# Last four experts that write finished rows, 64-row products in half chunks and 16-token tiles paired, in a one-core float32 hybrid layer

## The reference

```python
n = rms_norm(h, norm1_g)
u = n @ w_in
h = h + (sigmoid(g0) * (y_rwkv @ w_p_rwkv)       # 384 channels
       + sigmoid(g1) * (y_sb   @ w_p_sb)         # 320 channels
       + sigmoid(g2) * (y_fox  @ w_p_fox)) @ w_out   # 320 channels
t = rms_norm(h, norm2_g)
g_idx = argmax(t @ wg + bg)                      # one of 4 groups
top_v, top_i = top_k(le_sel, 2)                  # two of the 4 experts in that group
for e in range(16):
    he = silu(t @ w_gate[e]) * (t @ w_up[e])
    y = y + combine[:, e:e + 1] * (he @ w_down[e])
out = h + y
```

## Time and profile before

| | |
|---|---|
| median of 3 runs | 1109.23 us (1108.11 to 1111.26) |
| profiled execution, its own time | 1108.83 us |
| its span in the profile | 1107.0 us |
| mean granted TensorE clock | 0.956 of full speed |
| PE / PEld busy | 1012.5 us (91%) / 597.7 us (54%) |
| DVE / ACT / POOL busy | 317.9 / 211.6 / 84.8 us |
| moved by DMA | 111.52 MB |

### The profile page before, as it was taken

The page is one execution under the profiler, slowest core; times in us unless marked ns, Lnnn a source line. Parts: engine busy times, 40 slices in busy tenths (PEclk is TensorE's granted clock), DMA queues, the critical chain, the costliest instruction groups (busy, mean ns, idle before and its releaser), DMA issues.

```text
span 1107.0 us, 15412 instructions
## 1 busy us (share of the span) xinstructions
PE 1012.5 (91%) x6388; PEld 597.7 (54%) x6388; DVE 317.9 (29%) x672; ACT 211.6 (19%) x462; POOL 84.8 (8%) x196
## 2 busy tenths in 40 slices
PE   5997998998998879999999999999999669999992
PEld 4885776876766644555554444443345434444441
DVE  3213553223123157222222333333310342212110
ACT  4002321120210252233320000060012201101100
POOL 7700000000000000000000000000000011121211
PEclk9997999999999999999998999999999779999997
DMA  7212012101000200311110111043360347999994
GB/s 200 62 58 76 1 41 37 50 3 50 2 2 2 60 1 20 96 39 38 38 38 19 39 38 38 1 173 92 114 247 38 152 152 221 345 350 340 358 283 115
DMA packets 104262, 111.52 MB, mean 101 GB/s; under 512 B 16305, under 2 KB 93233, under 8 KB 104129
## 3 DMA queue, kind: packets, MB, share of 16 engines
q1 hardware_dynamic: 99584, 93.76, 26.4%
q0 software_dynamic: 4608, 16.78, 6.0%
HBM read 97.40 MB, written 15.20 MB: 102 GB/s over the span
## 4 chain that ended last, share of the span: by engine, by line
PE 87%; DVE 5%; issue 3%; ACT 2%; DMA 2%; SPq 0%; POOL 0%; DVEq 0%; POOLq 0%; ACTq 0%
PE ps L1356 15%; PE ps L1571 10%; PE ps L1258 8%; PE ps L1204 7%; PE ps L1185 7%; PE ps L1498 6%; PE ps L1528 5%; PE ps L1585 5%; PE ps L1209 5%; PE ps L1424 2%; PE ps L1457 2%; PE ps L1458 1%; PE ps L1563 1%; PE ps L1483 1%; PE ps L1435 1%
## 5 line engine op out<-in xcount | busy, mean ns | idle before, releaser
L1356 PE MATMUL ps<-arena 128*128 128x512 f32 x384 | 185.1, 623 | 1.0 <-ACT yT_all L626 0.3
L1356 PEld LDWEIGHTS ps<-arena 128*128 128x128 f32 x384 | 71.2, 197 | 73.3 <-issue 72.0
L1258 PE MATMUL ps<-arena 64*64 64x64 f32 x2376 | 82.3, 223 | 12.6 <-DVE arena L861 10.8
L1258 PEld LDWEIGHTS ps<-arena 64*64 64x64 f32 x2376 | 75.3, 137 | 33.5 <-issue 25.5
L1204 PE MATMUL ps<-arena 128*128 128x264 f32 x320 | 84.4, 408 | 0.0
L1571 PE MATMUL ps<-arena 128*128 128x512 f32 x176 | 78.7, 598 | 2.0 <-issue 1.9
L465 POOL DMA_INDIRECT arena<-n_rows,idx x16 | 15.6, 978 | 842.0 <-DVE idx L1067 834.1
L1185 PE MATMUL ps<-arena 128*128 128x264 f32 x320 | 73.1, 388 | 1.2 <-PE ps L1185 1.2
L1498 PE MATMUL ps<-yT_all,arena 128*128 128x512 f32 x144 | 68.0, 614 | 0.0
L1185 PEld LDWEIGHTS ps<-arena 128*128 128x128 f32 x320 | 60.6, 191 | 13.5 <-issue 2.8
L1204 PEld LDWEIGHTS ps<-arena 128*128 128x128 f32 x320 | 59.5, 195 | 12.4 <-issue 0.7
(11 more groups left out here) (318 smaller groups left out, 1103.5 us busy)
## 6 DMA issues: line engine op xcount, KB each, us to landing
arena<-in_moe_w_down SPq DMA_DIRECT2D x16, 1024.0 KB, 13.1
arena<-in_w_in SPq DMA_DIRECT2D x24, 512.0 KB, 3.9
arena<-in_moe_w_gate SPq DMA_DIRECT2D x11, 1024.0 KB, 14.4
arena<-in_moe_w_up SPq DMA_DIRECT2D x11, 1024.0 KB, 17.6
arena<-in_w_in SPq DMA_DIRECT2D x9, 1024.0 KB, 5.3
yT_all<-in_moe_w_gate SPq DMA_DIRECT2D x5, 1024.0 KB, 14.6
yT_all<-in_moe_w_up SPq DMA_DIRECT2D x5, 1024.0 KB, 17.0
arena<-in_w_out SPq DMA_DIRECT2D x1, 4096.0 KB, 13.5
```

The costliest lines, as they stand in the source:

```text
L1258: ins = mm(psf[q, 512 * bank + c * CH:512 * bank + (c + 1) * CH], lhs(q, c), rhs(q, c), start=True, stop=True)
L1356: ins = mm(ps[:, 5 + 2 * (n % 2), :], gate_w[:, (n + 1) % 4, c, :], nT[:, c, META:L], start=(c == 0), stop=(c == DC - 1))
```

## The change

1. **V tiles.** The four 128-token tiles of both pieces come first. The two 16-token tiles become one last group, "tail", of 16 steps: in each pair of steps one product goes to PSUM partitions 0 to 15 (320 columns) and one to 32 to 47 (325 columns), of the same bank.
2. **Projection.** Six banks instead of two. In each block, the seven products with 128 rows come first; then the two 64-row chunks as four products of 256 tokens, b = 1 and b = 2 in turn.
3. **Experts in time.** `ORDER` = 0, 4, 8, 12, 1, 5, 9, 13, 2, 6, 10, 14, 3, 7, 11, 15. The last four belong to four different groups.
4. **The end.** Twelve experts are added as before. When the twelfth has landed, ACT issues the copy of `y_dram` to `out`. For each of the last four, POOL gathers the rows so far from `y_dram` (`sums_in`), DVE multiplies and adds (`y_final`, two of 512 columns), and POOL writes the rows to `out` (`final_rows`), the first of them after the copy has landed.
5. **Other edits.** `down` signals its lower half by itself (`down_low`). `tables()` stands behind `rows_T(1)` and `gated(0)`, its two copies from PSUM before `rows_T(0)`. Head sums share two semaphores, and the wait for `qg8_ready` and `tilde_ready` go. The runtime loop follows the new scheme.

```diff
-        groups = [...] + [(N_SHIFT + 5 + f // 5, "v", f // 5, f % 5) for f in range(10)]
+        groups = [...] + [(N_SHIFT + 5 + f // 4, "v", f // 4, f % 4) for f in range(8)]
+        groups += [(N_SHIFT + 6, "tail", 0, 4)]
...
+                        if kind == "tail":
+                            k0, r = KT[k]
+                            mm(ps[0:r, b, 0:SW], nT[:, c, k0:k0 + r], slot(i - 1)[:, c, 0:SW], start=(c == 0), stop=(c == DC - 1))
+                            yield
+                            ins = mm(ps[32:32 + r, b, 0:RING_W], nT[:, c, k0:k0 + r], w[:, c, 0:RING_W], start=(c == 0), stop=(c == DC - 1))
...
-                    if n >= 2:
-                        pe.wait_ge(sem("proj_used"), n - 1)
-                    for c in range(3):
-                        rs = slice(0, P) if b == 0 or c < 2 else slice(64 * (b - 1), 64 * b)
-                        ins = mm(ps[:, 2 + n % 2, :], wpr[rs, dc % 2, 3 * b + c, :], yT[b][rs, c, :], start=(c == 0), stop=(c == 2))
+                    if n + b >= 6:
+                        pe.wait_ge(sem("proj_used"), n + b - 5)
+                    for c in range(3 if b == 0 else 2):
+                        ins = mm(ps[:, bank(b), :], wpr[:, dc % 2, 3 * b + c, :], yT[b][:, c, :], ...)
+                for k in range(2):
+                    for b in (1, 2):
+                        rs = slice(64 * (b - 1), 64 * b)
+                        cols = slice(256 * k, 256 * k + 256)
+                        ins = mm(ps[:, bank(b), cols], wpr[rs, dc % 2, 3 * b + 2, :], yT[b][rs, 2, cols], start=False, stop=True, ...)
...
-            for t in range(NT):
-                sp.dma_start(out[t * P:(t + 1) * P, :], y_dram[t * P:(t + 1) * P, :]).then_inc(sem("out_out"), 16)
...
+            pool.wait_ge(sem(f"y_out{(N_SUM - 1) % 3}"), 16 * (N_SUM // 3))
+            pool.sem_inc(sem("sums_done"), 1)
+            for t in range(N_SUM, N_SUM + 2):
+                sums_in(y_dram, dest[:, ORDER[t]:ORDER[t] + 1], t % 2)
+            for t in range(N_SUM, NE):
+                pool.wait_ge(sem("y_low"), t + 1)
+                pool.wait_ge(sem("y_high"), t + 1)
+                if t == N_SUM:
+                    pool.wait_ge(sem("out_out"), 16 * NT)
+                final_rows(ORDER[t], t % 3)
+                if t + 2 < NE:
+                    sums_in(y_dram, dest[:, ORDER[t + 2]:ORDER[t + 2] + 1], t % 2)
...
+                if t == N_SUM + 1:
+                    act.wait_ge(sem("sums_done"), 1)
+                    for i in range(NT):
+                        a.dma_start(out[i * P:(i + 1) * P, :], y_dram[i * P:(i + 1) * P, :]).then_inc(sem("out_out"), 16)
...
+            def y_final(t, s, ss, col):
+                for k, landed_, s_ in ((0, "down_low", "y_low"), (1, "down_psum", "y_high")):
+                    dve.wait_ge(sem(landed_), t + 1)
+                    cols = slice(512 * k, 512 * k + 512)
+                    stt(yo[:, s, cols], ps[:, 4 + k, :], coef[:, col:col + 1], so_far[:, ss, cols], ALU.mult, ALU.add).then_inc(sem(s_), 1)
...
             rows_T(0, 0, False)
-            tables()
             for t in range(NE + 1):
...
                     gated(t, t % 2, 2 + 4 * (t % 2))
...
+                if t == 0:
+                    tables()
```

More of the change, by code:

```diff
@@ L57 @@
 T_SPLIT = 4
+ORDER = [g * EPG + i for i in range(EPG) for g in range(NG)]
+N_SUM = NE - NG
 KT = [(128 * i, min(128, L - 128 * i)) for i in range(5)]
@@ L241, in slot_sem @@
             return sem(f"ring{i % RING}" if i < N_RING else f"late{(i - N_RING) % 2}")
-        groups = [(N_SHIFT + f // 4, "q", f // 2, f % 2) for f in range(20)] + [(N_SHIFT + 5 + f // 5, "v", f // 5, f % 5) for f in range(10)]
+        groups = [(N_SHIFT + f // 4, "q", f // 2, f % 2) for f in range(20)] + [(N_SHIFT + 5 + f // 4, "v", f // 4, f % 4) for f in range(8)]
+        groups += [(N_SHIFT + 6, "tail", 0, 4)]
         NF = len(groups)
+        STEPS = (NF + 1) * DC
         pe_order = []
@@ L534, in _ @@
             act.wait_ge(sem("params_in"), 320)
-            done(a.mul(qg8, qgc, 0.125), "qg8_ready")
+            done(a.mul(qg8, qgc, 0.125))
             n = 0
@@ L985, in _ @@
                     dst = merged[:, dc, :] if b == 0 else macc[:]
-                    done(tt(dst, gate(n), ps[:, 2 + n % 2, :], ALU.mult), "proj_used")
+                    done(tt(dst, gate(n), ps[:, (0, 1, 2, 3, 4, 6)[n % 6], :], ALU.mult), "proj_used")
                     if b > 0:
@@ L1150, in _ @@
                     gated(k + NE, 0, 2)
-                    y_high(k + NE, 0, NE, None)
+                    dve.wait_ge(sem("sum_in0"), k * 16 + 16 * 3)
+                    y_final(k + NE, 0, 0, NE)
         @block.tensor
```

133 lines of the change are left out of this document (78 added, 55 removed).

## The result

| | before | after |
|---|---|---|
| median of the runs | 1110.24 us (1108.11 to 1111.76, 4 runs) | 1094.22 us (1093.33 to 1095.18, 4 runs) |
| profiled execution, span | 1108.83, 1107.0 | 1095.18, 1093.4 |
| ratio after / before | | 0.9857, 95% interval 0.9835 to 0.9879 |

What follows compares the result with a forecast made beforehand. PE's own work was taken to bound the kernel, 87% of the chain of waits. Terms of -8.6, -3.5, -2.5 and -8.0 sum to -22.6 from 1108.83, giving 1086.2; forecast 1086.5 us, range 1080 to 1094.

Steps and rivals of the forecast that it cites:

- V filler: V tiles filling PE's waits in the recurrence: paired 16-token products take half the time, -3.5 us, between 0 and -4.5.
- The copy: Last experts: the copy of `y_dram` to `out` delays the last gate and up weights, PE stalls before `gate_up(15)`, +3.7 us.
- The half clock behind the output product's wait: After the projection: a 3 us wait may bring the half clock, up to 1.7 us, counted in the range only.
- Projection: Projection blocks: 64-row products on both array halves overlap, -10.0 us; DVE's later end gives back 1.4; term -8.6.
- First expert's end: Moving `tables()` back lets `gate_up(1)` start 2.0 us earlier, plus 0.5 of half clock: -2.5 us, between -1 and -3.5.
- The end: After the last expert's values: rows written without addition or a copy behind, span ending at 1095.3, -11.7 us if undisturbed.
- inside the same stall: Last experts: `down(13)`, perhaps 2 us late for its gather, adds nothing beside the 3.8 us stall for the weights.
- The copy disturbs nothing: Rival for the last experts: the weights keep their place despite the copy, -26.3 us in all, 1082.5; chance 0.20.
- no overlap: Rival for projection and filler: array halves take turns, 1096.5, or 1090 for columns only; chance 0.10 for both.
- strict order: Rival: records run in program order, 1.7 us more in the projection, some 2 more in the filler, 1090; chance 0.12.
- The end gives little: Rival for the end: weights and gathers late in turn, -2 us instead of -8, 1092.5; chance 0.10.
- POOL's queue behind the copy: Rival "slower": POOL's transfers wait behind a copy landing after 1104 instead of 1074; 1115 if at 1110; chance 0.03.

Runs made afterwards that it cites:

- order 1, 2, 0: The changed kernel with each projection block in the order branches 1, 2, 64-row pairs, branch 0: 1093.13 us, ratio 0.9845 to the kernel before.
- the best kernel: The changed kernel with the copy sent late and projection branches in order 1, 2, 0: 1083.75 us, ratio 0.977; again 1089.07, ratio 0.9794.
- experiment 2: The changed kernel without the copy of `y_dram` to `out` and the waits for it: 1089.38 us, one run.
- experiment 5: The changed kernel with the projection's 64-row products over 512 columns at once, not halves of 256 in turn: 1093.75 us, ratio 0.9848 to the kernel before.
- experiment 3: The changed kernel with experts 12 to 14 scaled out of PSUM at once, gathered rows added two turns later: 1096.91 us, ratio 0.9873 to the kernel before.

## Why the prediction was right, and where it failed

The steps that failed are three. The V filler's term left out the clock of the thin work behind it and is worth nothing on average instead of -3.5. The copy's term priced the wait for the weights, +3.7, where the wait for the gather ended last and brought the half clock: +7.2. The half clock behind the output product's wait was kept out of the sum and cost 1.7. The savings in PE's own work came out nearly as forecast.

- **Projection, -8.6.** Right in its mechanism, 1.9 short in its size. Full overlap of the two halves, 7.27 us a block, the wait near 3 us: each as worked out, -8.5 for the stretch. What failed is the sentence that the half clock of that wait "goes into the range" and not into the sum: it came, +1.7 at the output product, and order 1, 2, 0 takes it away. Total -6.7.
- **V filler, -3.5.** The step that failed is pricing PE's time alone. The pairs do run side by side, and save 3.3 us up to the chain's start at full clock, ACT's extra copy included (0.5, where I said 0.4). But I counted nothing for the clock behind: the stretch between has thin work, and in eight of ten profiles with pairs some 3 us more are lost in it. Averaged over runs the term can't be told from 0 (-0.4 us for the pairs alone, between -2.1 and +1.2; 0.2 us the other way in the best kernel). One pair of profiles shows +0.3 at the projection and the other -3.5, so one profile of each can't price it.
- **First expert's end, -2.5.** -3.6. The order of events was right (`gate_up(1)` 2.3 us nearer, 2.0 said); the half clock gave back 1.3 and not the 0.5 that I took, since PE's wait fell to 1.4 us.
- **The end, -11.7.** -10.7, right but for 1.0, by the traces; it has no experiment of its own. The last write goes out 0.9 us behind the last values, and lands in 3.2 to 6.6 us.
- **The copy, +3.7.** The mis-sized term: +7.2, of which 6.6 are the copy's by experiment 2. I named both victims and put them "inside the same stall". That held: they overlap. But I took the weights as the later one and a gather of 9.6 us as 2 us late. It took 11.1, POOL could issue it only at 1050.89, so `down(13)` waited 4.4 us, and the half clock came with the wait: 2.5 us more on `down(13)`, which no term had. Two premises were off: the copy's pieces are of 16 KB, not 32 (128 packets for 2.10 MB on its queue), and the DMA share isn't full at 1.12, it reaches 1.20 between 1054 and 1058.
- **The rivals.** "The copy disturbs nothing" and "no overlap" fell at once, strict order with the starts inside a pair and in experiment 5. "The end gives little" gave 1092.5 for a gain of 2 at the end; the end gave 3.5, and this came nearest, though by the gather and not by gathers and weights in turn. POOL's queue behind the copy hurt nobody.
- **Sum.** The misses are +1.9, +3.8, -1.1, +1.0, +3.5 and -0.1 between them: 9.0, from the -22.6 of the forecast to -13.6 in the two profiles. In the medians, 16.0 us apart, 6.6 are missing. The half clock makes 6.8 of the 9.0: 1.7 at the output product, 2.6 in and behind the chain, 2.5 at `down(13)`.

## What to carry to other kernels

In this kernel a saving on TensorE counted only with the clock of what came behind: where a shorter stretch leaves a wait of 3 us or thin work, charge the half clock in the sum, and price such a place by many runs, not by one profile of each. A bulk copy that is needed only at the end should wait for the last transfers that the engines wait for; moving it 13 us later made this kernel 5.9 us faster, for 0.4 us at the end. When several transfers compete, ask which is needed first: here it was the small gather that the buffers hung on, not the largest load.

## What the runs showed of the hardware that I had not expected

- One program's half-clock stretches are not in one place: 7 us between the chain's start and the first gate products in one execution of the kernel before, 17 us at the same instructions in the next, while the two executions differ by 2 us (1108.83 and 1110.9), since other stretches are shorter in turn.
- Four 64-row records of 512 columns, two for rows 0 to 63 and then two for rows 64 to 127, take 1.13 us, just as eight of 256 columns in turn.
- Of two products whose weights are 16 columns wide, on PSUM partitions 0 to 15 and 32 to 47, the second starts 0.01 us behind the first, ahead of the first's own second record.
- A 2 MB copy from memory to memory lengthens an indirect gather beside it from 6.95 to 11.1 us, and the landing of the last weights from 19.8 to 25.1 us after their issue (26.2 in experiment 3, where `gate_up(15)` waits 5.8 us for them).
